# Expert matrices of a two-layer diffusion backbone, loaded as halves of 2 MB in place of quarters of 1 MB

## The chip, the cores and the metric

The kernel runs on one NeuronCore of a Trainium2 chip, as one launch. All data are fp32. The metric is the device time of a run in microseconds (us), the median of several; before the change it is 1920.0 us (three runs, 1916.11 to 1920.92). Engines are named as in the profile: PE (matmuls; PEld its weight loads), DVE (VectorE), ACT (ScalarE), POOL (GpSimd) and SP (SyncE, which here only issues DMAs).

## The reference

Two layers over 256 context and 256 latent tokens of width 1024. Each layer is a token mixer (three branches, gated and merged, then one output product) and then a mixture of experts, which is what the change is about:

```python
def expert_choice_ffn(h, w_router, w1, w3, w2):          # 16 experts, D_EXPERT = 1024
    cap = EC_FACTOR * n // N_EXPERTS                      # 32 tokens for an expert
    aff = softmax((h @ w_router), axis=-1)
    g, idx = lax.top_k(swapaxes(aff, 1, 2), cap)
    xs = h[bidx, idx]
    hid = silu(xs @ w1[e]) * (xs @ w3[e])                 # for each expert e
    y = (hid @ w2[e]) * g
    return zeros_like(h).at[bidx, idx].add(y)

# around it, for each layer and stream (latent; context too in layer 0)
x = x + gt1 * rmsnorm(mixer(...), g_post1)
h2 = rmsnorm(x, g_pre2) * (1 + sc2) + sh2
x = x + gt2 * rmsnorm(expert_choice_ffn(h2, ...), g_post2)
```

An expert has three matrices of 1024 x 1024 (4 MB each): 192 MB a layer, 384 MB in all, each read once. Layer 0 runs both streams (64 token columns for an expert), layer 1 the latent one alone (32).

## The kernel before, in words

Every engine has its own program, written out in order, and semaphores tie them together. SP's list of loads (`issue_order`) is one queue: an item that waits holds up everything behind it.

**The ring.** Weights go into 8 ring places of 8 KB a partition (1 MB each), in turn. PE takes loads in a fixed order (`next_slot`); `weights_used` counts the loads it is through with, and `PREVIOUS[n]` is the load that had load n's place before. A load into the ring waits until that one is used (L456). An expert is 12 loads of 1 MB, j = 0 to 191 in `EXPERT_LOADS`: quarters of the first and second matrix for expert e, and then of the third for expert e-1. A quarter q is 256 rows of the matrix, two neighbouring rows to a partition (8 KB in one piece).

**Spare places.** While the mixer still runs, buffers that have become free take some of the first loads (`SPARE`: 8 of them in layer 0, 12 in layer 1), so that with the ring 16 or 20 expert loads can land before expert 0 starts. Each has its own condition (`spare_free`). From then on all loads go through the ring.

**The order in front of the experts of layer 0** is, in `issue_order`: the four w_out blocks; four `mod4` loads (rows of w_mod for the next modulation group, put into the places mix0 to mix3 for a while); four expert loads into the ring; the other four `mod4` loads, into the same places, each as DVE is through with the one before; five expert loads into spare places; four into the ring; three into spare places; and then the rest. The four w_out blocks are used up only in the output product's last chunk: L1159 gives back the first three as it begins the block after each, the last at its end.

**What DVE does there**, in this order (L2079 on): `mod4_part` 0 to 3, the post-norm and residual of token chunk 0 (L2051, L2053), `mod4_part` 4 and 5, chunk 1, `mod4_part` 6 and 7, chunk 2, copies of the first two turned chunks (L2062), chunk 3. A `mod4_part` waits for its load. After that come the router's logits, the ranking of tokens, the gather of the first group's tokens (L1254) and expert 0.

**PE with an expert** (L1321, L1347): the tokens are the stationary operand (64 or 32 columns), the matrix rows the moving one, in tiles of 512 columns (layer 0) or 256 (layer 1) side by side in the array. The k-th slice of the features of the gathered tokens has to match the rows that lie in partition p: `paired(k)` takes every second feature of a block of 256, for the rows turned by L732 (token rows, hidden units) and for the gather.

Of the kernel before, what the change touches and what calls it, by code (L numbers as in the profile page):

```python
# [19 lines left out]
P = 128  # L20
# [169 lines left out]
for _l in range(2):  # L190
# [3 lines left out]

SPARE = [{2: "mix0", 5: "mix1", 8: "mix2", 11: "mix3", 14: "yg", 17: "xst1", 20: "ya0", 23: "ya1"},
         {2: "ctx_rows", 5: "mixer_consts", 8: "old_rows", 11: "ya0", 14: "mix0", 17: "yg", 20: "mix1", 23: "mix2",
          26: "mix3", 29: "merged_end", 32: "ya1", 35: "gains"}]
SPARE_ORDER = [[2, 5, 8, 11, 20], [23, 14, 17], [2, 5, 8, 11], [14, 20, 23, 26], [29, 32, 17, 35]]  # L200
SLOT_OF, PREVIOUS, USE = [], [], []


def _assign_slots():

    turn, last, count = 0, {}, {f"mix{i}": 2 for i in range(4)}
    for l in range(2):
        spare = [None] * len(ring_loads(l)) + [SPARE[l].get(j) for j in range(len(EXPERT_LOADS))]
        for name in spare:
            slot = name  # L210
            if name is None:
# [5 lines left out]
            USE.append(count[slot])  # L217


_assign_slots()  # L220
# [25 lines left out]
def backbone(nc, x, c, ctx, c_ctx, w_mod, b_mod, g_pre1, g_post1, g_pre2, g_post2, w_in, g_q, g_kv, w_uq, w_ukv,  # L246
             rpb, b_ml_gates, g_ml, w_br_mla, w_br_na, w_br_ml, w_out, w_router, w_e1, w_e3, w_e2, rope, out):
    with ExitStack() as stack:
# [152 lines left out]
            return spare_slots[s] if isinstance(s, str) else ring[:, s, :]  # L401

        def landed(n):
            return sem(f"weights_landed_{SLOT_OF[n]}")

        used = sem("weights_used")
        small = sem("small_loaded")
# [5 lines left out]
        def _(sp):  # L413
# [44 lines left out]
            for l in range(2):  # L458
                n_ring, n_expert = BASE[l], BASE[l] + len(ring_loads(l))
                for (kind, lw, *a), j in issue_order(l):  # L460
# [21 lines left out]
                    if kind == "mod":  # L482
                        load(n, w_slot(n), w_mod[lw, a[1] * P:(a[1] + 1) * P, a[0] * SLOT:(a[0] + 1) * SLOT])
                    elif kind == "in":
                        load(n, w_slot(n)[:, 0:KD * a[1]].rearrange("p (k n) -> p k n", k=KD),
                             w_in[lw, :, a[0]:a[0] + a[1]].rearrange("(k p) n -> p k n", p=P))
                    elif kind == "out":
                        load(n, w_slot(n).rearrange("p (k n) -> p k n", k=KD),
                             w_out[lw, :, a[0] * BLK:(a[0] + 1) * BLK].rearrange("(k p) n -> p k n", p=P))
                    else:  # L490
                        e, m, q = a
                        load(n, w_slot(n), (w_e1, w_e3, w_e2)[m][l, e].rearrange("(q p k) n -> q p (k n)", q=4, p=P)[q])
                    if j is None:
                        n_ring += 1
            for s in range(2):
# [6 lines left out]
        def _(pool):  # L502
# [94 lines left out]
            params(0)  # L597

            def router_load(l):
                for q in range(4):  # L600
                    pool.dma_start(wrt[:, 2 * q:2 * q + 2, 0:N_EXP],
                                   w_router[l, 2 * q * P:2 * (q + 1) * P, :].rearrange("(p k) n -> p k n", k=2))\
                        .then_inc(sem("router_loaded"), 16)

            def gates_weights(l):
# [68 lines left out]
            def router_weights(l):  # L674


                pool.wait_ge(sem("router_loaded"), 64 * (l + 1))
# [43 lines left out]
        def _(pe):  # L721
# [55 lines left out]
            def mod_turn(o):  # L777
                l, g = MOD_GROUPS[o]
                src = mod_tmp[:, :] if g == 0 else gate_row(l, g)
                pe.wait_ge(sem("mod_row"), o + 1)  # L780
                if o:
                    pe.wait_ge(sem("mod_col"), o)
                for b in range(4):
                    cols = slice(128 * b, 128 * b + 128) if g == 0 else paired(b)
# [53 lines left out]
            for l, L in enumerate(layers):  # L838
# [341 lines left out]
                def turn_rows(j):  # L1180
# [4 lines left out]
                        pe.wait_ge(sem("xt_act"), before("xt_act", l) + j - 1)  # L1185
                        pe.wait_ge(sem("xt_dve"), before("xt_dve", l) + j - 1)
                    for k in range(KD):
                        mm = transpose(ps[:, b + k // 4, k % 4 * P:(k % 4 + 1) * P], X[:, t, paired(k)], P)
# [53 lines left out]
                def gather(g, pieces):  # L1242
# [4 lines left out]
                    for b, si in pieces:  # L1247
# [3 lines left out]
                        for i in range(4):  # L1251
                            k = 4 * b + i
                            for c2 in range(2):
                                mm = pe.matmul(ps[:, 4 + 2 * s + b, i * P:(i + 1) * P], X[:, 2 * s + c2, paired(k)],  # L1254
                                               Srs[l][:, si, c2, :], start=c2 == 0, stop=c2 == 1)
                        mm.then_inc(sem("gathered"), 1)

# [46 lines left out]
                def expert_in(e, m):  # L1304

                    for q in range(4):
# [11 lines left out]
                        for k in range(2):  # L1318
                            kk = 2 * q + k
                            for j in range(NT):  # L1320
                                mm = pe.matmul(ps[M * j:M * j + M, m, 0:NW], XSTs[l][e // GROUP % 2][:, kk, e % GROUP, 0:M],  # L1321
                                               w[:, k, j * NW:(j + 1) * NW], start=kk == 0, stop=kk == KD - 1)
                        mm.then_inc(used, 1)

                def turn_units(e):

                    pe.wait_ge(sem("hid_ready"), before("hid_ready", l) + e + 1)
                    for b in range(nb):
                        mm = transpose(ps[:, 2, b * P:(b + 1) * P], hids[l][:, paired(b)], P)
                    mm.then_inc(sem("hid_tr"), 1)  # L1330

                def expert_out(e):
# [979 lines left out]
```

## Time and profile before

| | |
|---|---|
| median of three runs | 1920.0 us (1916.11 to 1920.92) |
| the profiled execution, its own time | 1922.65 us |
| its span | 1920.9 us |
| busy: PE / DVE / ACT / POOL | 1685.3 / 591.1 / 327.2 / 95.1 us |
| moved by DMA | 525.16 MB, mean 273 GB/s |
| granted TensorE clock, mean | 0.947 of full |
| expert loads | 384, 1024 KB each; for the 364 into the ring a median of 17.8 us from issue to landing |

The span falls into four stages: the mixer of layer 0 (to about 627 us), its experts (to about 1085), the mixer of layer 1 (to about 1469) and its experts (to the end). Rates of the DMA queues and PE's busy share mean different things in each, so they are read by stage. A landing time in the profile is counted from SP's issue; with a full queue most of it is waiting behind other loads.

### The profile page before, as it was taken

The numbers are of one execution on the slowest core, as the hardware profiler recorded it, in microseconds if no ns is written. First come the engines' busy times: TensorE is split into PE (matmuls) and PEld (weight loads), VectorE is DVE, ScalarE is ACT, GpSimd is POOL, SyncE is SP. The second block draws the span as 40 slices with busy tenths as digits, with TensorE's granted clock in tenths as the row PEclk, the third lists the DMA queues.
The fourth block names the chain that finished last, engine by engine and source line by source line (L and its number), as shares of the span: only waits on it lengthen the run. The fifth ranks groups of instructions, "written<-read, shape, count | busy, mean of one in ns | idle before, by whom it ended". The sixth has DMA issues, their size and how long they took to land.

```text
span 1920.9 us, 21659 instructions
## 1 busy us (share of the span) xinstructions
PE 1685.3 (88%) x9131; PEld 879.3 (46%) x9131; DVE 591.1 (31%) x1082; ACT 327.2 (17%) x784; POOL 95.1 (5%) x174
## 2 busy tenths in 40 slices
PE   5999999999998998979889899999998766675666
PEld 2656445444476442423322366777885323232222
DVE  3744334364654112112121413444413111010101
ACT  3113334200023110100001321343012000000001
POOL 5001100000021000000000000110000000000000
PEclk9999999999999999999999999999999878787778
DMA  9631005153576899999999921207957999999996
GB/s 357 209 124 39 1 1 197 45 187 122 172 310 234 325 392 421 421 421 421 422 421 421 351 65 45 39 14 265 324 213 319 420 421 421 421 421 421 421 421 273
DMA packets 130668, 525.16 MB, mean 273 GB/s; under 512 B 9886, under 2 KB 73532, under 8 KB 75276
## 3 DMA queue, kind: packets, MB, share of 16 engines
q1 hardware_dynamic: 127884, 520.47, 68.7%
q0 software_dynamic: 2688, 3.32, 1.0%
q8 instruction: 72, 1.18, 0.3%
q14 instruction: 24, 0.20, 0.0%
HBM read 522.70 MB, written 1.05 MB: 273 GB/s over the span
## 4 chain that ended last, share of the span: by engine, by line
PE 62%; DMA 33%; DVE 3%; ACT 1%; issue 1%; SPq 0%; DVEq 0%; ACTq 0%
DMA ring<-in_w_e_dram 32%; PE ps L820 14%; PE ps L1121 10%; PE ps L1321 8%; PE ps L1159 4%; PE ps L1130 4%; PE ps L1347 4%; PE ps L1081 4%; PE ps L1043 2%; PE ps L732 2%; PE ps L941 2%; PE ps L1254 2%; DMA ring<-in_w_mod_dram 1%; PE ps L1065 1%; PE ps L1282 1%; PE ps L918 1%
## 5 line engine op out<-in xcount | busy, mean ns | idle before, releaser
L1321 PE MATMUL ps<-ring,arena 128*32 128x256 f32 (+1 forms) x2856 | 376.8, 504 | 109.7 <-DMA ring<-in_w_e_dram 106.8
L1321 PEld LDWEIGHTS ps<-ring,arena 128*32 128x32 f32 (+1 forms) x2856 | 122.3, 128 | 344.1 <-DMA ring<-in_w_e_dram 175.7
L1347 PE MATMUL ps<-ring,arena 128*32 128x256 f32 (+1 forms) x1496 | 213.2, 552 | 67.0 <-DMA ring<-in_w_e_dram 65.5
L1121 PE MATMUL ps<-arena,ring 128*128 128x512 f32 (+1 forms) x576 | 191.8, 486 | 0.0
L820 PE MATMUL ps<-arena,ring 128*128 128x512 f32 (+1 forms) x480 | 176.8, 524 | 0.0
L1347 PEld LDWEIGHTS ps<-ring,arena 128*32 128x32 f32 (+1 forms) x1496 | 68.5, 139 | 208.1 <-issue 107.2
L2178 DVE COPY arena<-ps 32x512 f32<-32x512 f32 (+1 forms) x124 | 68.6, 554 | 281.9 <-PE ps L1347 280.7
L1121 PEld LDWEIGHTS ps<-arena,ring 128*128 128x128 f32 x576 | 109.1, 190 | 76.5 <-issue 68.3
L1694 ACT ACTIVATE arena<-ps 128x512 f32<-128x512 f32 (+1 forms) x32 | 15.7, 490 | 728.6 <-PE ps L1321 728.6
L2171 DVE TENSOR_TENSOR arena<-arena,ps 128x512 f32<-128x512 f32 (+1 forms) x32 | 17.7, 555 | 376.0 <-PE ps L1321 376.0
L820 PEld LDWEIGHTS ps<-arena,ring 128*128 128x128 f32 x480 | 89.8, 190 | 84.1 <-issue 80.3
L1402 ACT ACTIVATE arena<-ps 128x512 f32<-128x512 f32 (+6 forms) x166 | 79.9, 488 | 202.7 <-PE ps L1159 65.8
L1783 DVE SCALAR_TENSOR_TENSOR arena<-ring,cT,arena 128x2048 f32<-128x2048 f32 x49 | 113.3, 2348 | 1.1
L1130 PE MATMUL ps<-arena 128*128 128x512 f32 (+1 forms) x256 | 89.0, 486 | 1.0 <-DVE arena L2009 1.0
L820 PE MATMUL ps<-ring,arena 128*128 128x256 f32 x384 | 85.3, 381 | 0.0
L1159 PE MATMUL ps<-ring,arena 128*128 128x256 f32 x384 | 83.7, 380 | 1.1 <-DVE arena L2032 1.1
L1159 PEld LDWEIGHTS ps<-ring,arena 128*128 128x128 f32 x384 | 72.8, 190 | 13.0 <-DVE arena L2032 2.3
L1447 ACT ACTIVATE arena<-ps 128x256 f32<-128x256 f32 (+3 forms) x84 | 37.9, 459 | 236.3 <-PE ps L820 230.2
L820 PEld LDWEIGHTS ps<-ring,arena 128*128 128x128 f32 x384 | 72.2, 190 | 12.8 <-issue 3.3
L1081 PE MATMUL ps<-arena,ring 128*128 128x512 f32 (+1 forms) x192 | 73.5, 507 | 0.0
L732 PEld LDWEIGHTS ps<-ident,arena 128*128 128x128 f32 (+2 forms) x360 | 44.4, 158 | 54.6 <-issue 41.2
L732 PE MATMUL ps<-ident,arena 128*128 128x128 f32 (+2 forms) x360 | 59.5, 287 | 6.6 <-DVE arena L2002 2.6
(234 smaller groups left out, 1406.9 us busy)
## 6 DMA issues: line engine op xcount, KB each, us to landing
ring<-in_w_e_dram SPq DMA_DIRECT2D x364, 1024.0 KB, 17.8
ring<-in_w_in_dram SPq DMA_DIRECT2D x44, 1024.0 KB, 9.1
ring<-in_w_mod_dram SPq DMA_DIRECT2D x40, 1024.0 KB, 10.1
arena<-in_w_e_dram SPq DMA_DIRECT2D x17, 1024.0 KB, 7.5
ring<-in_w_out_dram SPq DMA_DIRECT2D x8, 1024.0 KB, 11.1
arena<-in_w_mod_dram SPq DMA_DIRECT2D x8, 1024.0 KB, 14.7
arena<-in_w_br_ml_dram SPq DMA_DIRECT2D x8, 512.0 KB, 6.1
arena<-in_w_br_mla_dram SPq DMA_DIRECT2D x8, 256.0 KB, 3.8
```

The costliest lines, as they stand in the source:

```text
L732: return pe.transpose(o, i, ident[0:n, 0:n])
L820: mm = pe.matmul(o(ps[:, PROJECTION_BANK[i], :]), a, b, start=k == 0, stop=k == len(pairs) - 1)
L941: mm = pe.matmul(ps[:, 5 + o % 2, ti * 129:ti * 129 + 129], E[u % 2][:, s, t * P:(t + 1) * P], mv1[:, s, h, :], start=j == 0, stop=j == le ...
L1081: mm = pe.matmul(ps[:, PROJECTION_BANK[g], tq], gate_w[0][:, k, (f % 2) * P:(f % 2 + 1) * P], hT[:, k, tq], start=k == 0, stop=k == KD - 1 ...
L1121: mm = pe.matmul(ps[:, u % 3, tq], wg[:, k, cols], hT[:, k, tq], start=k == 0, stop=k == KD - 1)
L1130: mm = pe.matmul(ps[:, 3 + u % 3, tq], wb[:, k0 + k, cols], src[:, k, tq], start=k == 0, stop=k == nk_ - 1)
L1159: mm = pe.matmul(ps[:, o % 6, 0:BLK], merged[:, k, t * P:(t + 1) * P], wo[nb][:, k, :], start=k == 0, stop=k == KD - 1)
L1321: mm = pe.matmul(ps[M * j:M * j + M, m, 0:NW], XSTs[l][e // GROUP % 2][:, kk, e % GROUP, 0:M], w[:, k, j * NW:(j + 1) * NW], start=kk == 0 ...
L1347: mm = pe.matmul(ps[M * j:M * j + M, 3, 0:NW], lhs, w[:, k, j * NW:(j + 1) * NW], start=kk == 0, stop=kk == KD - 1)
L1402: return act.activation(o, i, ACT.Copy)
L1783: ins = dve.scalar_tensor_tensor(out=acc[s], in0=w_slot(n), scalar=cT[:, k, s:s + 1], in1=acc[s], op0=ALU.mult, op1=ALU.add)
L2178: ins = dve.tensor_copy(Yg[ee * CAP:(ee + 1) * CAP, si, at:at + NW], ps[j * CAP:(j + 1) * CAP, 3, 0:NW])
```

## The change

- Expert matrices are cut into halves of 512 rows, four neighbouring rows to a partition: 16 KB in one piece. A half goes as one DMA of 2 MB into two neighbouring ring places, once both are free (`max` of the two `PREVIOUS`), and both quarters are signalled by one semaphore (`SIGNAL`). The last four loads of a layer, and those in spare places, stay DMAs of 1 MB with 8 KB in a piece.
- The spare places now hold both quarters of a half (j = 2, 3, 8, 9, ... in place of 2, 5, 8, 11, ...).
- Before a layer's first expert load, one ring place is left out if that is needed to start on an even one (it is, in both layers).
- Features and hidden units are dealt to partitions in fours: `in_fours(k)` takes every fourth feature of a block of 512. In layer 1 the moving operand takes columns in pairs, two of every four.
- The router's weights come in two DMAs in place of four, dealt in the same way.

```diff
-SPARE = [{2: "mix0", 5: "mix1", 8: "mix2", 11: "mix3", 14: "yg", 17: "xst1", 20: "ya0", 23: "ya1"},
...
-SPARE_ORDER = [[2, 5, 8, 11, 20], [23, 14, 17], [2, 5, 8, 11], [14, 20, 23, 26], [29, 32, 17, 35]]
+SPARE = [{2: "mix0", 3: "mix1", 8: "mix2", 9: "mix3", 14: "yg", 15: "xst1", 20: "ya0", 21: "ya1"},
...
+SPARE_ORDER = [[2, 3, 8, 9, 20], [21, 14, 15], [2, 3, 8, 9], [14, 20, 21, 26], [27, 32, 15, 33]]
+def half_matrix(l, j):
+    first = j - j % 2
+    return first < len(EXPERT_LOADS) - 4 and first not in SPARE[l]
...
+            if j == 0:
+                turn += turn % 2
+            if slot is None:
                 slot, turn = turn % SLOTS, turn + 1
-            count[slot] = count.get(slot, 0) + 1
+            if j > 0 and j % 2 and half_matrix(l, j):
+                SIGNAL.append(SIGNAL[-1])
+            else:
+                SIGNAL.append(slot)
+                count[slot] = count.get(slot, 0) + 1
...
-                        load(n, w_slot(n), (w_e1, w_e3, w_e2)[m][l, e].rearrange("(q p k) n -> q p (k n)", q=4, p=P)[q])
+                        w = (w_e1, w_e3, w_e2)[m][l, e].rearrange("(h p k) n -> h p k n", h=2, p=P)[q // 2]
+                        if half_matrix(l, j):
+                            if q % 2 == 0:
+                                sp.wait_ge(used, max(PREVIOUS[n], PREVIOUS[n + 1]) + 1)
+                                at = SLOT_OF[n]
+                                sp.dma_start(ring[:, at:at + 2, :].rearrange("p a n -> p (a n)"), w.rearrange("p k n -> p (k n)"))\
+                                  .then_inc(landed(n), 16)
+                        else:
+                            k = 2 * (q % 2)
+                            load(n, w_slot(n), w[:, k:k + 2, :].rearrange("p k n -> p (k n)"))
...
+                                if nb == 4:
+                                    cols = w[:, k, j * NW:(j + 1) * NW]
+                                else:
+                                    a = j % 2 * nb
+                                    cols = w[:, k, j // 2 * 512:j // 2 * 512 + 512].rearrange("p (c f) -> p c f", f=4)[:, :, a:a + nb]
                                 mm = pe.matmul(ps[M * j:M * j + M, m, 0:NW], XSTs[l][e // GROUP % 2][:, kk, e % GROUP, 0:M],
-                                               w[:, k, j * NW:(j + 1) * NW], start=kk == 0, stop=kk == KD - 1)
+                                               cols, start=kk == 0, stop=kk == KD - 1)
...
-                        mm = transpose(ps[:, 2, b * P:(b + 1) * P], hids[l][:, paired(b)], P)
+                        mm = transpose(ps[:, 2, b * P:(b + 1) * P], hids[l][:, b:P * nb:nb], P)
...
-def paired(b):
-    return slice(2 * P * (b // 2) + b % 2, 2 * P * (b // 2) + 2 * P, 2)
+def in_fours(b):
+    return slice(4 * P * (b // 4) + b % 4, 4 * P * (b // 4) + 4 * P, 4)
```

The places that the four `ring` loads ahead of expert 0 take, by `PREVIOUS` (counted back from j = 0, the four w_out blocks being -4 to -1): before, j = 0, 1, 3, 4 wait for -8, -7, -6, -5, and j = 6, 7, 9, 10 for -4 to -1. Now the pair 0, 1 waits for -6, the pair 4, 5 for -4, the pair 6, 7 for -2 and the pair 10, 11 for -1. It is the same in both layers.

SP's queue in front of layer 0's experts, before (w_out blocks, `mod4` loads into the arena, expert loads of 128x2048):

```order
L456 DMA ring<-in_w_out_dram 128x8x256 [waits weights_used] x4
L466 DMA arena<-in_w_mod_dram 128x2048 [waits mg_branch] x4
L456 DMA ring<-in_w_e_dram 128x2048 [waits weights_used] x4
L466 DMA arena<-in_w_mod_dram 128x2048 [waits mod_part,mg_branch] x4
L456 DMA arena<-in_w_e_dram 128x2048 [waits mod_part,mg_branch] x4
L456 DMA arena<-in_w_e_dram 128x2048 [waits x_post1]
L456 DMA ring<-in_w_e_dram 128x2048 [waits weights_used] x4
```

And now:

```order
L468 DMA ring<-in_w_out_dram 128x8x256 [waits weights_used] x4
L478 DMA arena<-in_w_mod_dram 128x2048 [waits mg_branch] x4
L509 DMA ring<-in_w_e_dram 128x4096 [waits weights_used] x2
L478 DMA arena<-in_w_mod_dram 128x2048 [waits mod_part,mg_branch] x4
L468 DMA arena<-in_w_e_dram 128x2048 [waits mod_part,mg_branch] x4
L468 DMA arena<-in_w_e_dram 128x2048 [waits x_post1]
L509 DMA ring<-in_w_e_dram 128x4096 [waits weights_used] x2
```

No item moved against the others: four ring loads became two of 128x4096 at the same place, between the two groups of `mod4` loads.

SP's queue in front of layer 1's experts, before:

```order
L456 DMA ring<-in_w_out_dram 128x8x256 [waits weights_used] x4
L456 DMA rows<-in_w_e_dram 128x2048 [waits mod_tr]
L456 DMA arena<-in_w_e_dram 128x2048 [waits merged]
L456 DMA ring<-in_w_e_dram 128x2048 [waits weights_used] x4
L456 DMA arena<-in_w_e_dram 128x2048 [waits mg_branch] x4
L456 DMA ring<-in_w_e_dram 128x2048 [waits weights_used] x4
L456 DMA arena<-in_w_e_dram 128x2048 [waits wo_ready]
```

And now:

```order
L468 DMA ring<-in_w_out_dram 128x8x256 [waits weights_used] x4
L468 DMA rows<-in_w_e_dram 128x2048 [waits mod_tr]
L468 DMA arena<-in_w_e_dram 128x2048 [waits merged]
L509 DMA ring<-in_w_e_dram 128x4096 [waits weights_used] x2
L468 DMA arena<-in_w_e_dram 128x2048 [waits mg_branch] x4
L509 DMA ring<-in_w_e_dram 128x4096 [waits weights_used] x2
L468 DMA arena<-in_w_e_dram 128x2048 [waits wo_ready]
```

Here too the pairs stand where the single loads stood, ahead of four spare places (mix0 to mix3).

## Rows read from the trace of the kernel before

**Rows 1.** The page's chain that ended last, shares of the span by engine.

```profile
PE 62%; DMA 33%; DVE 3%; ACT 1%; issue 1%; SPq 0%; DVEq 0%; ACTq 0%
```

**Rows 2.** Busy time by stage: window, length, engines, clock, DMA share, GB/s.

```profile
690.00:1060.00 370.00, 331.88 (x1482) 116.22 (x1480) 67.73 (x112) 29.79 (x63) 4.78 (x12) 1.00 1.01 421
1500.00:1890.00 390.00, 257.96 (x2682) 103.63 (x2678) 42.47 (x98) 13.42 (x36) 4.16 (x7) 0.78 1.01 421
```

**Rows 3.** SP's issues before expert 0 of layer 0: start, length, what, count.

```profile
536.29 1.98 SPq L456 DMA_DIRECT2D ring<-in_w_e_dram  x4
540.92 9.98 SPq L466 DMA_DIRECT2D arena<-in_w_mod_dram  x4
...
586.15 10.35 SPq L456 DMA_DIRECT2D ring<-in_w_e_dram  x4
...
628.89 2.04 SPq L456 DMA_DIRECT2D ring<-in_w_e_dram  x2
```

**Rows 4.** DVE in the same stretch: products, post-norm, copy of turned rows, last residual.

```profile
570.62 1.28 DVE L2051 SCALAR_TENSOR_TENSOR arena<-arena,stat 128x1024 f32<-128x1024 f32 x1 [3.46 <-ACT stat L1407]
...
573.20 5.58 DVE L1798 SCALAR_TENSOR_TENSOR arena<-arena,cT 128x512 f32<-128x512 f32 x8
...
598.10 0.69 DVE L2062 COPY arena<-ps 128x512 f32<-128x512 f32 x1 [11.05 <-PE ps L732]
...
600.91 1.23 DVE L2053 TENSOR_TENSOR X<-X,arena 128x1024 f32<-128x1024 f32 x1
```

**Rows 5.** PE: first turned rows, first gather and expert 0 of layer 0.

```profile
596.88 2.08 PE L732 MATMUL ps<-ident,X 128*128 128x128 f32 x16
...
619.18 7.80 PE L1254 MATMUL ps<-arena,X 128*128 128x128 f32 x64 [0.46 <-ACT arena L1671]
626.91 3.65 PE L1321 MATMUL ps<-ring,arena 128*64 128x512 f32 x16
```

**Rows 6.** DMA view of 1000 to 1050 us, and of 1080 to 1090.

```profile
DMA packets 2890, 21.05 MB, mean 421 GB/s; under 512 B 322, under 2 KB 322, under 8 KB 322
q1 hardware_dynamic: 2888, 21.02, 101.1%
...
DMA packets 3456, 3.50 MB, mean 350 GB/s; under 512 B 50, under 2 KB 3455, under 8 KB 3455
q1 hardware_dynamic: 3455, 3.49, 109.6%
```

**Rows 7.** DMA view of 585 to 588 us: one load on an idle queue.

```profile
ring<-in_w_e_dram SPq DMA_DIRECT2D x1, 1024.0 KB, 4.9
```

**Rows 8.** By stage, as rows 2: an idle stretch of PE and the next.

```profile
1101.00:1104.00 3.00, 1.03 (x9) 0.84 (x9) 3.00 (x11) 2.66 (x8) 0.75 (x4) 1.00 0.12 37
1104.00:1107.00 3.00, 2.11 (x13) 1.81 (x12) 1.96 (x6) 0.86 (x3) 0.00 (x0) 0.60 0.00 0
```

**Rows 9.** PE: four loads of layer 0, and one of layer 1 at the lower clock.

```profile
1076.28 7.09 PE L1347 MATMUL ps<-ring,arena 128*64 128x512 f32 x32
...
1895.73 1.94 PE L1347 MATMUL ps<-ring,arena 128*32 128x256 f32 x16 [0.56 <-DMA ring<-in_w_e_dram]
```

**Rows 10.** SP's issues before expert 0 of layer 1.

```profile
1416.56 2.09 SPq L456 DMA_DIRECT2D ring<-in_w_e_dram  x4
1418.70 1.95 SPq L456 DMA_DIRECT2D arena<-in_w_e_dram  x4
1435.92 10.35 SPq L456 DMA_DIRECT2D ring<-in_w_e_dram  x4
...
1470.31 8.96 SPq L456 DMA_DIRECT2D ring<-in_w_e_dram  x8
```

**Rows 11.** By stage, as rows 2: the two stops of the queues in layer 1.

```profile
1395.00:1417.00 22.00, 20.93 (x98) 18.10 (x97) 3.80 (x9) 3.20 (x6) 0.00 (x0) 1.00 0.00 1
1463.00:1471.00 8.00, 8.00 (x78) 6.24 (x80) 4.10 (x15) 0.69 (x2) 0.80 (x2) 1.00 0.01 2
```

**Rows 12.** The gather's weight loads and matmuls: duration min/median/max in ns, starts, forms.

```profile
L1254 PEld LDWEIGHTS ps<-arena,X x384: 193/196/331, 619.2 to 1726.8; 128*128 128x128 f32 x192
L1254 PE MATMUL ps<-arena,X x384: 281/281/422, 619.2 to 1727.0; 128*128 128x128 f32 x192
```

More of the change, by code:

```diff
@@ L192 @@
     _n += len(ring_loads(_l)) + len(EXPERT_LOADS)
-SPARE = [{2: "mix0", 5: "mix1", 8: "mix2", 11: "mix3", 14: "yg", 17: "xst1", 20: "ya0", 23: "ya1"},
-         {2: "ctx_rows", 5: "mixer_consts", 8: "old_rows", 11: "ya0", 14: "mix0", 17: "yg", 20: "mix1", 23: "mix2",
-          26: "mix3", 29: "merged_end", 32: "ya1", 35: "gains"}]
-SPARE_ORDER = [[2, 5, 8, 11, 20], [23, 14, 17], [2, 5, 8, 11], [14, 20, 23, 26], [29, 32, 17, 35]]
-SLOT_OF, PREVIOUS, USE = [], [], []
+SPARE = [{2: "mix0", 3: "mix1", 8: "mix2", 9: "mix3", 14: "yg", 15: "xst1", 20: "ya0", 21: "ya1"},
+         {2: "ctx_rows", 3: "mixer_consts", 8: "old_rows", 9: "ya0", 14: "mix0", 15: "yg", 20: "mix1", 21: "mix2",
+          26: "mix3", 27: "merged_end", 32: "ya1", 33: "gains"}]
+SPARE_ORDER = [[2, 3, 8, 9, 20], [21, 14, 15], [2, 3, 8, 9], [14, 20, 21, 26], [27, 32, 15, 33]]
+SLOT_OF, SIGNAL, PREVIOUS, USE = [], [], [], []
+def half_matrix(l, j):
+    first = j - j % 2
+    return first < len(EXPERT_LOADS) - 4 and first not in SPARE[l]
 def _assign_slots():
@@ L207, in _assign_slots @@
     for l in range(2):
[L208 to L211, printed above, removed]
-                slot, turn = turn % SLOTS, turn + 1
-            count[slot] = count.get(slot, 0) + 1
+        for i in range(len(ring_loads(l)) + len(EXPERT_LOADS)):
+            j = i - len(ring_loads(l))
+            slot = SPARE[l].get(j)
+            if j == 0:
+                turn += turn % 2
+            if slot is None:
+                slot, turn = turn % SLOTS, turn + 1
+            if j > 0 and j % 2 and half_matrix(l, j):
[3 more added lines that the diff above has]
+                count[slot] = count.get(slot, 0) + 1
+            USE.append(count[SIGNAL[-1]])
             PREVIOUS.append(last.get(slot))
@@ L216, in _assign_slots @@
             SLOT_OF.append(slot)
-            USE.append(count[slot])
 _assign_slots()
@@ L403, in landed @@
         def landed(n):
-            return sem(f"weights_landed_{SLOT_OF[n]}")
+            return sem(f"weights_landed_{SIGNAL[n]}")
         used = sem("weights_used")
@@ L599, in router_load @@
             def router_load(l):
-                for q in range(4):
-                    pool.dma_start(wrt[:, 2 * q:2 * q + 2, 0:N_EXP],
-                                   w_router[l, 2 * q * P:2 * (q + 1) * P, :].rearrange("(p k) n -> p k n", k=2))\
+                for h in range(2):
+                    pool.dma_start(wrt[:, 4 * h:4 * h + 4, 0:N_EXP],
+                                   w_router[l, 4 * h * P:4 * (h + 1) * P, :].rearrange("(p k) n -> p k n", k=4))\
                         .then_inc(sem("router_loaded"), 16)
@@ L674, in router_weights @@
             def router_weights(l):
-                pool.wait_ge(sem("router_loaded"), 64 * (l + 1))
+                pool.wait_ge(sem("router_loaded"), 32 * (l + 1))
                 pool.wait_ge(sem("mod_col"), 6 if l else 3)
@@ L783, in mod_turn @@
                 for b in range(4):
-                    cols = slice(128 * b, 128 * b + 128) if g == 0 else paired(b)
+                    cols = slice(128 * b, 128 * b + 128) if g == 0 else in_fours(b)
                     mm = transpose(ps[:, 7, 128 * b:128 * b + 128], src[:, cols], P)
@@ L1187, in turn_rows @@
                     for k in range(KD):
-                        mm = transpose(ps[:, b + k // 4, k % 4 * P:(k % 4 + 1) * P], X[:, t, paired(k)], P)
+                        mm = transpose(ps[:, b + k // 4, k % 4 * P:(k % 4 + 1) * P], X[:, t, in_fours(k)], P)
                         if k == 3:
@@ L1253, in gather @@
                             for c2 in range(2):
-                                mm = pe.matmul(ps[:, 4 + 2 * s + b, i * P:(i + 1) * P], X[:, 2 * s + c2, paired(k)],
+                                mm = pe.matmul(ps[:, 4 + 2 * s + b, i * P:(i + 1) * P], X[:, 2 * s + c2, in_fours(k)],
                                                Srs[l][:, si, c2, :], start=c2 == 0, stop=c2 == 1)
```

## Prediction

> **What bounds the kernel now.** I read the page's DMA slices and chain first. In the chain that ended last, a third is waiting for expert loads [rows 1]. The table by stage then shows two long stretches, one in each layer's experts, where the DMA queues are busy without a break at 421 GB/s, while PE has slack: 332 of 370 us in the first, 258 of 390 us in the second [rows 2]. In them the end is set by three things only: when the stream of loads (re)starts, how many bytes follow, and the rate. An earlier landing gives time one for one; a PE that starts late lets the stream restart late. Expert 0 finds its first loads already landed, and the loads after those wait for it to free places. So everything that SyncE does ahead of expert 0 has to be read too: its order of issues [rows 3], what DVE does in between [rows 4], and when PE starts expert 0 [rows 5].
>
> **The rate (gain).** A window in which nearly only 8 KB pieces move has 2888 packets in 50 us, 322 of them completion marks: 2566 pieces in 16 x 50 us, 311.8 ns each. A window of 1 KB pieces has 3455 packets, 50 small: 3405 in 16 x 10 us, 47.0 ns each [rows 6]. The line through both is 37.8 ns per KB and 9.2 ns per piece. A piece of 16 KB then takes 614 ns where two of 8 KB take 624, which is 0.037 us per MB of 2.49 (421 GB/s becomes 427). Layer 0 streams 192 - 16 = 176 MB after its restart, of which I count 168 (the last loads are quarters, and PE sets the end of that layer, below): 6.2 us. Layer 1 streams 192 - 20 = 172 MB, 164 counted: 6.1 us. **Gain 12.3 us.** Bounds: nothing, if the per-piece cost grows with the piece; and twice this, if what is saved is more than the line says (25 us).
>
> The Trainium skill, "DMA: Bandwidth & Descriptors", Specifications, puts the fabric's ceiling at 435 GB/s. By that figure no piece size could save more than 2.49 - 2.41 = 0.08 us per MB, some 27 us in all, and the sum below would be 1915. No run here shows that ceiling; 421 is what the rows have.
>
> **The blocked queue in layer 0 (loss, the largest term).** SyncE issues in order. Eight loads before expert 0 are the four w_out blocks in four ring places. Now j=0 and 1 take the places of the loads at -7 and -6, and j=4 and 5 those at -5 and -4, since the change also skips a place so as to start on an even one. Load -4 is the first w_out block. It is counted as used when the last chunk of the output product has begun its second column block; j=6 (place of -4 before) was issued on just that, at 586.15 [rows 3]. Before, the four ring loads needed only -8 to -5 and went out at 536.29. Now the DMA for j=4 and 5 sits in SyncE's queue from about 537 to 586.15, and behind it stand the second four modulation loads (mod4, k=4 to 7; before at 540.92) and the first five spare loads.
>
> Who waits for those: DVE, in order. Its program is products k=4,5, post-norm of chunk 1, products k=6,7, post-norm of chunk 2, two copies of turned rows, post-norm of chunk 3. A single load on an idle queue takes 4.9 us [rows 7]. The pair goes first (4.9 us of transfer), so k=4 lands at 586.15 + 4.9 + 4.9 = 596.0, the next at 598.4, 600.9, 603.4. DVE takes 5.58 / 2 = 2.8 us for a k, 573.20 - 570.62 = 2.6 for a post-norm, 0.7 for a copy [rows 4]. So: 598.8, 601.6, post-norm 604.2, 607.0, 609.8, post-norm 612.4, copies 613.8, post-norm 616.4. Before, the last ended at 600.91 + 1.23 = 602.14. That is 14.2 us; what follows (router, ranking, gather at 619.18, expert 0 at 626.91 [rows 5]) hangs on it serially. **Loss 14 us.** The spare loads land by about 634, ahead of a PE that starts at 641, so they add nothing.
>
> **A colder PE in that gap (loss).** PE turned the first rows at 596.88 [rows 5] and will have little work until 613. After a thin stretch of 1.03 us in 3 the granted clock fell to 0.60 in this trace, and stayed at 0.5 beyond [rows 8]. Some 6 us of PE work on the router's chain could run at half speed: 0 to 6 us, I take **2**, as it rises again after some us of work.
>
> **Coarser places (loss).** The first load that restarts the stream went out at 628.89, one load after PE's start. A pair needs both places: one load more, which is 7.09 / 4 = 1.8 us in layer 0 [rows 9], 0.9 in layer 1 (half of the 1.93 us below at the fast clock). While PE frees places in the ramp, pairs of 4.9 us with 2.4 us of latency leave the queues idle somewhat more than single loads do: I followed the first 12 pairs with 1.72 us per load, and get 0.7 us more in layer 0, none in layer 1. At each end PE starts on a pair only when both halves are there, so that it finishes the last pair one load later: 1.8 us in layer 0, where the end is PE's (32 matmuls, turns and sums after load 183), and between 1.0 and 1.9 us in layer 1, by the clock [rows 9], say 1.3. **Loss 1.8 + 0.9 + 0.7 + 1.8 + 1.3 = 6.5 us.** In mid-stream the coarser grain costs nothing: three pairs, 6 MB or 14.7 us of transfer, stay queued while PE takes 3.5 us for the fourth.
>
> **The same block in layer 1 (no loss).** j=4,5 now wait for the use at 1435.92 and the four spare loads behind them too, which before went at 1418.70 [rows 10]. Before, the queues stood still until 1417, ran 18 MB until 1463 and stood again until 1471 [rows 11], since the next issue waits for PE (1470.31). Now they stop after 3 MB and run the other 14 MB from 1437 to 1471. The hole moves, and what it costs is under 1 us, which lies in the 0.9 above. No mod4 loads stand in this queue.
>
> **Free edits.** The router's two DMAs instead of four land hundreds of us ahead of use. In layer 1 the moving operand of the expert matmuls now reads two of every four columns; PE has slack there [rows 2], and would need 2.5 us per MB in place of 0.9 before it counted; at the end it could cost some us (in the range). Weight loads of rows (and of layer 0's units) step by 4 elements in place of 2. The step of 2 took 196 ns in the gather [rows 12]; no row has a step of 4. Between no cost and a doubled load it is 0 to 18 us: 32 turned and 64 gathered loads lie on layer 0's path at about 0.12 us of pace, and half as many on layer 1's. I take nothing.
>
> **Sum.** -12.3 + 14 + 2 + 6.5 = +10.2 us. The profiled execution took 1922.65 against the median of 1920.0, so the sum is laid on the median: **1930 us**.
>
> **Rivals.**
> - *The block in SyncE's queue is hidden (not slower).* The late post-norms would be absorbed before expert 0. Then the 14 + 2 us go, and the time is 1914; with the rate gain at its upper bound it is 1901. For it: DVE and PE are both idle in places there. Against it: DVE's one long idle stretch, 11.05 us before the first copy [rows 4], is used up in the working above, and behind it all is serial. It comes out faster from the point where block and cold clock together cost nothing at the line's rate, or under 12 us at the bound. Chance 0.16: 0.11 faster, 0.05 the same.
> - *A 16 KB piece is no cheaper per byte.* For it: nothing in the trace moves such pieces into these places, and the engines may lose on a larger piece what they save. Then 1942. Chance 0.19.
> - *Weight loads at a step of 4 elements are slow.* 16 bytes between elements; the price is up to 18 us, all of it outside the DMA-bound stretches: 1948. For it: one element of four is used where it was one of two. Against it: a turned load has 0.28 us of matmul beside it [rows 12], so it may be covered. Chance 0.09. The Trainium skill, "SBUF — State Buffer", Door 1 (the note on cachelines), says that reads run at full rate with at least two hits on a 16-byte line, which a step of 2 has and a step of 4 hasn't; the same note calls a stride of 4 fp32 free, so by its rule it could go either way, and no row here shows the step.
> - *Forecast*, chance 0.56, its own range 1922 to 1938: 0.42 slower, 0.14 the same (the terms of 12.3 and 14 nearly cancel, so 4 us less loss is already no change).
>
> **Numbers.** 0.3% (5.8 us) is about what a measurement can tell from no change. Faster 0.11, the same 0.19, slower 0.70. The range takes in part of both sides: 1913 to 1946.
>
> **What would show it.** Right: SyncE's issues of the second four w_mod loads at 586 to 588 in place of 541 to 551; no transfer between 550 and 587; DVE's products k=4 to 7 at about 596 to 610; expert 0 at 641 in place of 627; in layer 1 no transfer between about 1440 and 1451 (the old 1426 to 1437, moved by the delay) and none missing just before expert 0; 427 GB/s in the expert stages. Wrong: a rate of 421 (second rival), weight loads of X well over 196 ns (third), or expert 0 near 627 with the rest as said (first).

## The result

| | median | ratio to before, 95% interval |
|---|---|---|
| before | 1920.46 us (1916.11 to 1923.06, 4 runs) | |
| after | 1952.74 us (1949.06 to 1957.16, 4 runs) | 1.0172 (1.0157 to 1.0188) |

The change costs 32 us. The forecast was +10 us (1930), with a range of 1913 to 1946, so the measured time lies above its upper end. The profiled execution after has a span of 1955.0 us, 34.2 above the one of before.

### The profile page after: what moved, and what is told of

Read it like the earlier page. It is cut to its first block, busy times and chain, and to the rows that moved or that the text cites. A ratio compares the mean times of both kernels' runs of the same rounds, so it can differ in the third digit from the quotient of the medians.

```text
span 1955.0 us, 21477 instructions
## 1 busy us (share of the span) xinstructions
PE 1706.7 (87%) x9131; PEld 942.5 (48%) x9131; DVE 590.8 (30%) x1082; ACT 327.1 (17%) x784; POOL 92.2 (5%) x170
## 4 chain that ended last, share of the span: by engine, by line
PE 68%; DMA 27%; DVE 3%; ACT 1%; issue 1%; SPq 0%; DVEq 0%; ACTq 0%
DMA ring<-in_w_e_dram 25%; PE ps L841 13%; PE ps L1347 11%; PE ps L1142 10%; PE ps L1373 5%; PE ps L1151 4%; PE ps L1275 4%; PE ps L1180 4%; PE ps L1102 3%; PE ps L753 2%; PE ps L1064 2%; PE ps L962 2%; DMA ring<-in_w_mod_dram 1%; PE ps L1086 1%; PE ps L1303 1%; PE ps L939 1%
## 5 line engine op out<-in xcount | busy, mean ns | idle before, releaser
L1347 PE MATMUL ps<-ring,arena 128*32 128x256 f32 (+1 forms) x2816 | 358.4, 504 | 103.3 <-DMA ring<-in_w_e_dram 96.5
L1347 PEld LDWEIGHTS ps<-ring,arena 128*32 128x32 f32 (+1 forms) x2816 | 129.4, 127 | 312.9 <-issue 164.4
L1373 PE MATMUL ps<-ring,arena 128*32 128x256 f32 (+1 forms) x1536 | 201.1, 530 | 70.7 <-DMA ring<-in_w_e_dram 69.2
L1373 PEld LDWEIGHTS ps<-ring,arena 128*32 128x32 f32 (+1 forms) x1536 | 76.5, 136 | 191.0 <-issue 130.2
L2197 DVE TENSOR_TENSOR arena<-arena,ps 128x512 f32<-128x512 f32 (+1 forms) x32 | 17.7, 554 | 369.9 <-PE ps L1347 369.9
L1428 ACT ACTIVATE arena<-ps 128x512 f32<-128x512 f32 (+6 forms) x166 | 79.8, 488 | 194.1 <-PE ps L1180 55.4
L1275 PEld LDWEIGHTS ps<-arena,X 128*128 128x128 f32 x384 | 91.1, 328 | 10.7 <-issue 9.6
L1275 PE MATMUL ps<-arena,X 128*128 128x128 f32 x384 | 94.2, 401 | 0.5 <-ACT arena L1697 0.5
```

The lines of the kernel that those rows point to most:

```text
L1373: mm = pe.matmul(ps[M * j:M * j + M, 3, 0:NW], lhs, w[:, k, j * NW:(j + 1) * NW], start=kk == 0, stop=kk == KD - 1)
L1428: return act.activation(o, i, ACT.Copy)
```

## The profile after

The starts and ends of the expert stages (first and last matmul of the expert lines in the trace) place the loss:

| us | expert 0 of layer 0 | its stage | then to expert 0 of layer 1 | its stage |
|---|---|---|---|---|
| before | 626.9 | 456.5 | 385.8 | 439.4 |
| after | 658.1 | 463.0 | 389.4 | 432.3 |
| difference | +31.2 | +6.5 | +3.6 | -7.1 |

So nearly all of it stands ahead of layer 0's first expert. SyncE's issues there (columns: start, length, engine, line, what, count) answer to [rows 3]:

```profile
536.38 50.19 SPq L509 DMA_DIRECT2D ring<-in_w_e_dram  x2
586.68 1.95 SPq L478 DMA_DIRECT2D arena<-in_w_mod_dram  x4
599.02 11.72 SPq L468 DMA_DIRECT2D arena<-in_w_e_dram  x5
610.79 1.12 SPq L509 DMA_DIRECT2D ring<-in_w_e_dram  x2
621.28 13.16 SPq L468 DMA_DIRECT2D arena<-in_w_e_dram  x3
```

The row at 536.38 is 50.19 us long: its first pair went out at once, its second at 586.24, and the four w_mod loads came right behind, at 586.68 in place of 540.92. DVE in the same stretch, as in [rows 4]:

```profile
596.21 5.58 DVE L1824 SCALAR_TENSOR_TENSOR arena<-arena,cT 128x512 f32<-128x512 f32 x8 [36.64 <-DMA arena<-in_w_mod_dram]
601.71 1.28 DVE L2077 SCALAR_TENSOR_TENSOR arena<-arena,stat 128x1024 f32<-128x1024 f32 x1
...
604.28 5.58 DVE L1824 SCALAR_TENSOR_TENSOR arena<-arena,cT 128x512 f32<-128x512 f32 x8
...
616.47 0.69 DVE L2088 COPY arena<-ps 128x512 f32<-128x512 f32 x1 [4.15 <-PE ps L753]
...
620.02 1.23 DVE L2079 TENSOR_TENSOR X<-X,arena 128x1024 f32<-128x1024 f32 x1
```

DVE waits 36.64 us for the first of these loads. Products and post-norms then follow as the prediction had them (596.21, 601.71, 604.28). But the first copy starts at 616.47, 4.15 us after DVE was free, and the last residual ends at 621.25, not at 616.4. PE, as in [rows 5], and the clock by stage:

```profile
614.38 3.69 PE L753 MATMUL ps<-ident,X 128*128 128x128 f32 x16 [17.26 <-ACT arena L1428]
...
642.94 7.27 PE L1275 MATMUL ps<-arena,X 128*128 128x128 f32 x30 [0.46 <-ACT arena L1697]
...
658.07 3.65 PE L1347 MATMUL ps<-ring,arena 128*64 128x512 f32 x16
```

```profile
596.00:614.00 18.00, 0.82 (x5) 0.52 (x4) 15.79 (x20) 5.97 (x17) 0.00 (x0) 0.60 0.98 391
614.00:637.00 23.00, 19.23 (x118) 12.66 (x119) 10.04 (x24) 8.32 (x20) 2.97 (x4) 0.50 0.82 323
637.00:643.00 6.00, 5.54 (x18) 2.65 (x16) 4.92 (x16) 1.28 (x4) 0.00 (x0) 1.00 0.68 279
```

PE turns the first rows at 614.38, where it had done so at 596.88, because it waits for ACT. What ACT itself waits for in these microseconds is DVE's post-norms (its own rows; L1446 takes a norm statistic, L1428 copies a block that PE has made):

```profile
604.28 1.06 ACT L1446 ACTIVATE arena<-X 128x1024 f32<-128x1024 f32 x1 [24.99 <-DVE X L2079]
...
612.35 1.06 ACT L1446 ACTIVATE arena<-X 128x1024 f32<-128x1024 f32 x1 [3.52 <-DVE X L2079]
...
613.96 0.36 ACT L1428 ACTIVATE arena<-ps 128x256 f32<-128x256 f32 x1
```

From about 599 to 637 us PE's clock is the lower of the two, 1.2 GHz. That is how 602.14 became 621.25, and how the router's chain from there to the gather took 21.7 us in place of 17.0. Then the gather itself: from 642.94 to 658.07, 15.1 us in place of 7.7. Its weight loads, as in [rows 12]:

```profile
L1275 PEld LDWEIGHTS ps<-arena,X x384: 307/329/332, 642.9 to 1768.8; 128*128 128x128 f32 x192
```

A load of 128 columns takes 329 ns in place of 196 at a step of 4 elements. The same is seen in layer 1, where the gather took 7.7 us in place of 4.0; that is the +3.6 in the first table.

The rate rose as forecast in layer 1, and not in layer 0. By stage, as in [rows 2]:

```profile
720.00:1060.00 340.00, 311.86 (x1368) 128.59 (x1366) 64.31 (x107) 25.82 (x58) 4.79 (x12) 1.00 1.00 420
1530.00:1880.00 350.00, 229.43 (x2518) 116.80 (x2518) 44.37 (x104) 11.28 (x31) 4.16 (x7) 0.82 1.01 427
```

427 GB/s in layer 1 for 421. In layer 0 it is 420, with a DMA share of 1.00 for 1.01. There the slow gathers and the pairs of places get in each other's way. In x2_step2 and x3_both (below), with weight loads at a step of 2, the same window of layer 0 shows 427; in x5_gather_step4, with slow gathers but DMAs of 1 MB, it shows 421 as before.

## The experiments

All times are medians; a difference is against before as run on the same chips (1919.0 to 1921.2 us).

**x1_order: the queue reordered.** In layer 0 the pair j = 4, 5 goes out behind the loads that DVE waits for.

```diff
-        order += mods[:4] + ring[:4] + mods[4:] + pick(SPARE_ORDER[0]) + ring[4:8] + ...
+        order += mods[:4] + ring[:2] + mods[4:] + pick(SPARE_ORDER[0]) + ring[2:8] + ...
```

> The changed kernel with SyncE's queue reordered in layer 0 alone: the second pair of ring loads (j = 4, 5) goes out after the second four mod4 loads and the first five spare loads, not ahead of them. Theory (the block in SyncE's queue costs what stands between 602.14 and 621.25 us, 19 us, and another 5 us by a PE at half clock until 637): 1952.7 - 24 = 1929 us, expert 0 of layer 0 at about 634 in place of 658. The prediction's own size of the block (14 + 2): 1937. Rival (the weight loads at a step of 4 elements carry the loss, the late products hardly): above 1945.

Measured: 1932.5 us, ratio 1.006 (1.004 to 1.0079); expert 0 at 634.3. The reordering gives back 20 us, 4 less than the theory had. The rival above 1945 is out.

**x2_step2: weight loads at a step of 2.**

```diff
-                        mm = transpose(ps[:, b + k // 4, k % 4 * P:(k % 4 + 1) * P], X[:, t, in_fours(k)], P)
+                        mm = transpose(ps[:, b + k // 4, k % 4 * P:(k % 4 + 1) * P], X[:, t, paired(k)], P)
...
-                                mm = pe.matmul(ps[:, 4 + 2 * s + b, i * P:(i + 1) * P], X[:, 2 * s + c2, in_fours(k)],
+                                mm = pe.matmul(ps[:, 4 + 2 * s + b, i * P:(i + 1) * P], X[:, 2 * s + c2, paired(k)],
...
-                        mm = transpose(ps[:, 2, b * P:(b + 1) * P], hids[l][:, b:P * nb:nb], P)
+                        mm = transpose(ps[:, 2, b * P:(b + 1) * P], hids[l][:, paired(b)], P)
```

> The changed kernel with the weight loads of the turned rows, of the gather and of the hidden units stepping by 2 elements as before, so that features meet the wrong matrix rows (another result, the same work). Theory: the gather in front of expert 0 gets 7.5 us back in layer 0 and 3.7 us in layer 1, and the three further gathers of layer 0 some of the 6.5 us that its expert stage became longer: 1952.7 - 11 - (4 to 8) = 1934 to 1938 us. Rival (the block explains nearly all of the loss and slow weight loads lie beside matmuls): 1950.

Measured: 1932.5 us, 1.006 (1.0037 to 1.0083), expert 0 of layer 0 at 651.2. This too gives back 20 us, slightly more than the theory had. Layer 0's expert stage fell from 463.0 to 453.3 us.

**x3_both: both edits.** Like every kernel here whose steps don't match the transfers, it computes another result by the same work.

> The changed kernel with both edits: the reordered queue, and weight loads that step by 2 elements (another result, the same work). What is left of the change is the transfers themselves: 2 MB in pieces of 16 KB, a pair of places for each. Theory (427 GB/s for 421 gives 12 us, coarser places take 6): 1920.5 - 6 = 1914 us, and expert stages of about 450 and 432 us. Rival (nothing gained by larger pieces): 1924 to 1927.

Measured: 1913.21 us, 0.9956 (0.9941 to 0.9971): faster than before. Expert 0 starts at 626.9 as before, the stages take 452.6 and 436.1 us. The transfers, with their coarser places, are worth 7 us. The three numbers add up: -7 + 20 + 20 = +33, and after has +32. Each edit is worth 20 us while the other cause is there and 19 once it is gone, so neither hides behind the other.

**x4_block: the block alone, put into the kernel before.**

```diff
+                    if l == 0 and j == 3:
+                        sp.wait_ge(used, BASE[0] + len(ring_loads(0)) - 4 + 1)
```

> The kernel before with one wait more in SyncE's queue: the third of the four ring loads ahead of expert 0 in layer 0 waits until the first w_out block is used, as the changed kernel's second pair does. All transfers and steps are those of before. Theory: expert 0 of layer 0 24 us late (19 us by the late products and the ACT and DVE work behind them, 5 by PE's clock), 1920.5 + 24 = 1944 us. The prediction's size: 1936. Rival (the block is hidden): 1920.

Measured: 1941.56 us, 1.0106 (1.0088 to 1.0124); expert 0 at 648.0, 21.1 us late. So the block alone costs 21 us, 3 less than the theory and 5 more than the prediction's own size. In this trace SyncE's wait ended at 587.93, 1.8 us later than the same condition before (586.15), since the stretch ahead of it ran late; 19.3 of the 21.1 us lie behind it. The clock was back at full speed at 621, and the chain from the last residual (622.78) to the gather (640.25) took 17.5 us. In the traces of after and of x2_step2, with the same block, the clock came back only at 637 and the chain took 21.6 to 21.7; why it came back at different times isn't known.

**x5_gather_step4: the gather's step alone, in the kernel before.**

```diff
-                                mm = pe.matmul(ps[:, 4 + 2 * s + b, i * P:(i + 1) * P], X[:, 2 * s + c2, paired(k)],
+                                mm = pe.matmul(ps[:, 4 + 2 * s + b, i * P:(i + 1) * P], X[:, 2 * s + c2, in_fours(k)],
```

> The kernel before, with one edit: the gather's weight loads of X step by 4 elements in place of 2 (features meet the wrong matrix rows: another result, the same work). Theory (a step of 4 makes each such load 329 ns for 196 and the gather's pace 0.24 us for 0.12): expert 0 starts 7.5 us later in layer 0 and 3.7 us later in layer 1, and layer 0's expert stage grows by up to 8 us by its three further gathers: 1920.2 + 11 + (2 to 8) = 1934 to 1939 us. Rival (the turned rows and hidden units at a step of 4 carry it, or the load lies beside its matmul): 1920 to 1925.

Measured: 1938.26 us, 1.0092 (1.0075 to 1.0109). Expert 0 is 7.4 us late in layer 0; layer 1's gather adds 3.7 (4.0 to 7.7 us); layer 0's expert stage grew from 456.5 to 462.8. The gather's row, and then the first 90 us of that stage, counted from the start of expert 0, in the kernel before and in this one:

```profile
619.15 15.20 PE L1254 MATMUL ps<-arena,X 128*128 128x128 f32 x64 [0.46 <-ACT arena L1671]
634.28 3.65 PE L1321 MATMUL ps<-ring,arena 128*64 128x512 f32 x16
```

```profile
626.90:716.90 90.00, 90.00 (x449) 36.01 (x450) 15.31 (x32) 8.93 (x21) 5.11 (x5) 1.00 0.94 366
```

```profile
634.30:724.30 90.00, 90.00 (x415) 40.89 (x416) 13.13 (x28) 8.93 (x21) 5.11 (x5) 1.00 0.87 338
```

The pace of a matmul is 15.20 / 64 = 0.24 us in place of 0.12. In the ramp PE is busy all the time and sets the pace at which ring places come free. The second gather falls into it, in four pieces that take 7.3 us more of PE's time than before, and the queues move 338 GB/s in place of 366: 2.5 MB less, which is 6.0 us at 421 GB/s. In the 90 us after that both kernels move 421 GB/s, although the third gather is as slow. So what was lost in the ramp is what comes out at the end, as 6.3 us.

**x12_turned_step4: the other strided loads, in the kernel before.** Turned token rows and layer 0's hidden units at a step of 4, the gather at 2.

> The kernel before with the weight loads of the turned token rows and of the hidden units at a step of 4 elements (layer 1's units keep 2, as in the changed kernel), the gather as before (another result, the same work). Theory (only the gather loads weights for every matmul at a pace that the load sets; 32 and 16 turned rows cost little): 1920.8 + 0 to 2 us. Rival (each strided load costs 0.13 us on the path wherever it stands, 48 on it here before the experts and 8 for each expert in layer 0): 1930.

Measured: 1920.24 us, 1.0004 (0.9994 to 1.0015): nothing. The weight loads of the 48 turned rows kept their 209 ns (median); the kernel before, and then this one:

```profile
L732 PEld LDWEIGHTS ps<-ident,X x48: 194/209/265, 596.8 to 1451.7; 128*128 128x128 f32 x48
```

```profile
L732 PEld LDWEIGHTS ps<-ident,X x48: 196/209/261, 597.3 to 1448.9; 128*128 128x128 f32 x48
```

**x6_pairs_8k: 2 MB in a DMA, but 8 KB in a piece.** Everything of x3_both but the dealing of rows, which is in pairs again, and what hangs on it (the router's DMAs, layer 1's moving operand).

```diff
-                                sp.dma_start(ring[:, at:at + 2, :].rearrange("p a n -> p (a n)"), w.rearrange("p k n -> p (k n)"))\
+                                sp.dma_start(ring[:, at:at + 2, :], (w_e1, w_e3, w_e2)[m][l, e].rearrange("(h a p k) n -> h p a (k n)", h=2, a=2, p=P)[q // 2])\
```

> DMAs of 2 MB into pairs of places as in the changed kernel, queue reordered in layer 0, but each DMA in pieces of 8 KB: two neighbouring rows to a partition, steps of 2 elements, all as before. Against x3_both (1913.2 us) only the piece differs. Theory (the gain is a fixed cost per piece of 9 ns): rate 421 to 422 GB/s, 1913.2 + 11 = 1924 us, 4 slower than before by the coarser places. Rival (the gain comes from fewer and larger DMAs): 427 GB/s and 1913 us.

Measured: 1922.12 us, 1.0011 (1.0000 to 1.0022), 9 us above x3_both. The DMA view of 1700 to 1750 us, of x3_both and then of this kernel:

```profile
DMA packets 1465, 21.37 MB, mean 427 GB/s; under 512 B 161, under 2 KB 161, under 8 KB 161
q1 hardware_dynamic: 1463, 21.33, 100.4%
```

```profile
DMA packets 2723, 21.03 MB, mean 421 GB/s; under 512 B 159, under 2 KB 159, under 8 KB 159
q1 hardware_dynamic: 2720, 20.98, 100.8%
```

21.33 MB in 1463 packets against 20.98 MB in 2720, in the same 50 us. The gain is the piece's, not the DMA's size. With larger DMAs alone the coarser places are what is left: 1.5 us above before, by the interval between nothing and 4.

**x9, x10, x11: what the block is made of.** x9_block_warm adds to x4_block 64 matmuls that nobody reads, ahead of the first turned rows; x10_block_act moves ACT's norm statistics of chunks 1 and 2 behind its last copies; x11_block_both does both.

```diff
+                    for _ in range(64):                                                      # x9, x11 (PE)
+                        pe.matmul(ps[:, 7, 0:P], ident[:, :], ident[:, :], start=True, stop=True)
-                        if j and nb == 3:                                                    # x10, x11 (ACT)
+                        if j and nb == 3 and (l or j == 1):
+                if l == 0:                                      # behind the last chunk
+                    for j in (2, 3):
+                        act.wait_ge(sem("x_post1"), before("x_post1", l) + j)
+                        norm_stat(2, L.chunks[j - 1], junk_y)
```

> x4_block with 64 idle matmuls (128 columns, nobody reads them) on PE ahead of layer 0's first turned rows, so that PE is busy in the gap that the block opens. Theory (a part of the block's 21 us is PE's clock at half rate while it turns the first rows, 3.69 us for 16 matmuls where 2.08 is usual): granted clock 1.0 at 616 us, expert 0 some 2 us earlier than in x4_block, 1941.6 - 2 = 1939 to 1940 us. Rival (the clock costs nothing there, DVE and ACT set the pace): 1941.6. If the idle matmuls end after 616 us they cost time themselves, and the time is above 1942.

> x4_block with one more edit: in layer 0, ACT takes the norm statistics of token chunks 1 and 2 after it has copied all blocks of the output product, not before the fourth block of the next chunk. ACT then no longer stands at DVE's late post-norms with PE's output still to copy. Theory (the 5 us by which the block exceeded the sum of DVE's late products are this wait: PE turned its first rows at 616 in place of 597 because ACT copied the last blocks late): the last post-norm ends about 4 us earlier, 1941.6 - 4 = 1937 to 1938 us. Rival (DVE's own queue sets the pace, the copies are beside it): 1941.6.

> x4_block with both edits, the idle matmuls and the later norm statistics on ACT. What is then left of the block is DVE's own queue: products and post-norms behind loads that land at 596 to 603 us. Theory (the block costs 14 us on DVE, as the prediction worked out, and the other 5 to 7 by ACT's order and PE's clock, each of which hides the other's cure when cured alone): last post-norm at 616 to 618, expert 0 at 641 to 642, 1920.8 + 14 = 1935 us. Rival (the two cures do not add up, something else holds the chain): 1938 or more, as each alone.

Measured: x9 1939.6 us (1.0095, 1.008 to 1.011), x10 1938.26 (1.0082, 1.0064 to 1.0100), x11 1939.62 (1.0098, 1.0077 to 1.0119). By medians the first two come out near their theories, but their intervals reach into x4_block's, and x11 missed: 1935 was expected, and it came out where its rival had it (1938 or more). The traces say more than the times. In x11 DVE (first fence) did what the prediction's sum had, yet PE (second fence, by stage) lost its clock a little later:

```profile
604.49 5.58 DVE L1807 SCALAR_TENSOR_TENSOR arena<-arena,cT 128x512 f32<-128x512 f32 x8
...
615.64 1.22 DVE L2062 TENSOR_TENSOR X<-X,arena 128x1024 f32<-128x1024 f32 x1
```

```profile
598.00:611.00 13.00, 13.00 (x119) 13.00 (x118) 12.72 (x17) 2.24 (x8) 0.00 (x0) 1.00 0.99 392
611.00:617.00 6.00, 4.30 (x57) 3.54 (x56) 5.39 (x7) 3.01 (x8) 0.00 (x0) 1.00 0.97 385
617.00:631.00 14.00, 11.19 (x66) 7.02 (x67) 4.52 (x16) 4.87 (x11) 2.98 (x4) 0.51 1.01 407
```

The last residual ended at 616.86, where the forecast said 616.4. The clock, which in x4_block was down from 601, stood at 0.97 to 0.99 until 617 here; then it fell for 14 us, and the router's chain ran at half speed. It didn't have to: x9 has the same filler, PE was busy for still less of 611 to 617 us there (2.86 us, for 4.30 in x11), and its granted clock stayed at 1.00:

```profile
611.00:617.00 6.00, 2.86 (x32) 2.48 (x34) 2.37 (x4) 4.41 (x11) 0.00 (x0) 1.00 0.99 397
617.00:631.00 14.00, 9.75 (x103) 5.94 (x94) 8.66 (x23) 5.39 (x13) 2.97 (x4) 1.00 1.00 410
```

In x9 the last residual ended at 619.83 and the chain took 17.1 us, as before the change, so expert 0 was 17.8 us late. That is the block with ACT's wait and without the clock. In x10 DVE's last residual came at 617.60, 5.2 us before x4_block's 622.78, and the clock stood at 0.50 from 604 to 634 (x4_block: from 601 to 621). Expert 0 started at 648.5, no earlier, since the chain to the gather took 23.2 us. So ACT's wait is real, and in the profiled run the clock took back what its cure had given; whether it must isn't shown, as each kernel was profiled once. Expert 0 came at 644.7, 648.5 and 646.0 in x9, x10, x11 against 648.0.

**x7_layer1 and x8_layer1_w2: what can be kept.** x7 leaves layer 0 as before and changes layer 1 alone. x8 adds halves for the third matrix of experts 4 to 13 in layer 0 (its rows are hidden units, so no gather changes) and makes layer 1's last eight loads quarters.

```diff
+    if l == 0:
+        e, m, _ = EXPERT_LOADS[first]
+        return m == 2 and 4 <= e <= 13                        # x7: return False
+    return first < len(EXPERT_LOADS) - 8 and first not in SPARE[l]     # x7: - 4
...
+def dealt(l):
+    return in_fours if l else paired
```

> Layer 0 as before (quarters of 1 MB, features in pairs, the old order), layer 1 as in the changed kernel (halves of 2 MB, features in fours). Theory: layer 0 loses nothing; layer 1 starts its expert 0 some 4 us late by the gather at a step of 4, and wins 6 to 7 us in its stage: 1920.2 - 3 = 1917 us. Rival (the gather's loss in layer 1 outweighs the rate): 1922.

> As x7_layer1, with two additions: in layer 0 the third matrix of experts 4 to 13 comes in halves too (its rows are hidden units, so the gather keeps its step of 2), and in layer 1 the last eight loads are quarters, so that the end waits for single loads. Theory: 40 MB at 0.037 us each, 1.5 us, and some 1 us at the end: 1914 to 1915 us, faster than before. Rival (pairs among single loads leave the queues short, as a pair needs two places at once): 1918 or more.

Measured: x7 1918.83 us, 0.9995 (0.9986 to 1.0005), x8 1918.49 us, 0.9991 (0.9982 to 0.9999). In x7 layer 1's stage fell from 439.4 to 433.0 us and its gather took back 3.7; the time is 2 us above the theory. x8 missed its 1914 to 1915 and came out where its rival had it (1918 or more). It is the best version here with the right result, and it beats before by 0.1%, at the edge of what can be told. Its two additions aren't told apart from nothing. To keep x3_both's 7 us, X would have to lie in memory in the dealt order; that wasn't tried.

## Why the prediction was wrong

Term by term, as the prediction had them:

| term | forecast | measured | from |
|---|---|---|---|
| weight loads at a step of 4, "I take nothing" | 0 (bound 18) | +18 to +20 | x5_gather_step4; x2_step2 |
| the block on DVE, and PE's clock | +14 and +2 | +20 to +21 | x1_order; x4_block |
| rate, in both layers | -12.3 | -9 | x3_both against x6_pairs_8k |
| coarser places | +6.5 | +1.5 (0 to 4) | x6_pairs_8k |
| sum | +10.2 | +32 | |

**The step that failed is "Free edits".** There a load of 0.12 us of pace was priced between nothing and double, and set at nothing since "no row has a step of 4". In the gather it was double, 0.24 us, and that alone costs 18 us (x5_gather_step4). The rival for it, 1948 at a chance of 0.09, had the price right (18 us), partly by luck. It counted the turned loads, which cost nothing, and left out the later gathers of layer 0, one of which stands in the ramp and costs 6 us. Its reason against ("a turned load has 0.28 us of matmul beside it") rests on a row that is the gather's, and there such a matmul covered nothing. Turned rows did come out free, but that this is the reason isn't shown. No row of before told the two apart: the gather's loads stand at a pace of 0.12 us (64 in 7.80 us) and the turned ones at 0.13 (16 in 2.08 us), with 196 and 209 ns for a load.

**The block was right in mechanism and place, and too small by 5 us.** SyncE's queue and DVE's products came to within half a microsecond (596.21 for 596.0 in after), and so did the last post-norm where ACT was out of the way (616.86 in x11_block_both for 616.4). What was missing is that ACT has its own order too. Its norm statistics wait for DVE's post-norms, and behind them stand the copies of PE's last blocks, which PE waits for before it turns a row. The prediction named what is queued behind SyncE's wait, and not what is queued behind those of DVE. In x9_block_warm, whose clock never fell, expert 0 came 17.8 us late in place of the forecast 14.2, which is 3.6 for ACT. The clock term depends on the trace. Counted from the end of SyncE's wait (586.2 to 587.9) to expert 0, and against the 40.8 us of before, the delay is 17.7 us in x9, 19.3 in x4_block with the clock down until 621, and 23.8 in x2_step2 with the clock down until 637: so 1.6 to 6 us for the 2 that were taken. This is read from one trace of each kernel; the medians of x9 and x4_block differ by 2 us, and their intervals overlap.

**The rate was right, and its net gain came out near the forecast with some luck.** 421 became 427 GB/s, as the line through the pieces of 1 and 8 KB had it, and x6_pairs_8k shows that it is the piece. But both terms were too large: the rate gave 9 us of 12.3, and the coarser places cost 1.5 of 6.5. Their errors cancel, so that -5.8 and the measured -7 agree. Which of the five parts of the places' sum was too large isn't shown. That layer 0's rate would stay at 420 beside the slow gathers wasn't foreseen either. In layer 1 the block moved the hole in the transfers and cost nothing visible, as forecast. After, the queues stand still from 1433.0 to 1454.9 and from 1463.3 to 1474.7, and about the start of expert 0 (1510.5) for 2.2 us, where they had stood for 8.3. In x3_both, which keeps this block, the stretch between the two expert stages is 385.8 us as before.

The first rival (the block hidden) and the second (no gain by pieces) are both out.

## What to carry to other kernels

- When a transfer's layout changes, follow every reader of the data that has to match it. Here 9 us of rate (x3_both against x6_pairs_8k) were paid for with 18 to 20 in the gathers, whose operand X isn't part of the transfer at all.
- Where a load needs two places in place of one, look up which use frees the second, and list what stands behind it in the queue; then do the same once more for each engine that waits for one of those.
- A rate gain counts only while the queues are full. Here every PE delay ahead of the stream's restart came out at the end one for one (21.1 us late, 21 us longer in x4_block), and one in its ramp nearly so (7.3 us of PE's time, 6.3 at the end in x5_gather_step4).

## What the runs showed of the hardware

- An fp32 weight load of 128 columns for a matmul takes 196 ns at a step of 2 elements and 330 ns at a step of 4 (x5_gather_step4). For a turned block (a transpose against the identity) it stays at 209 ns at either step (x12_turned_step4). Why the two differ isn't known. One difference that the traces show: an fp32 matmul of the program is two loads and two matmuls in them (the 64 idle ones of x9_block_warm are 128 rows), a turned block one of each. The Trainium skill, "SBUF — State Buffer", Door 1 (the note on cachelines), asks for two hits on a 16-byte line and also calls a stride of 4 fp32 free: the gather's loads go by the first half of it, the turned rows' by the second.
- The moving operand of layer 1's expert matmuls, two of every four columns, cost little: 32 of them took 2.00 to 2.02 us after and 1.91 to 1.93 before, both 0.06 us each, in a stage where PE has slack.
- 16 KB pieces move at 427 GB/s into one core, 8 KB pieces at 421, and 8 KB pieces do so whether in DMAs of 1 MB (before) or of 2 MB (x6_pairs_8k).
